# A two-block transformer step on one core: layer-norm statistics by halves on VectorE, and two units of low halves given to GpSimd

## The chip, the cores and the metric

The kernel is one program on one core of one Trainium2 chip. The metric is the device time of one launch in microseconds. The core's engines each run an instruction stream of their own: TensorE (PE; its weight loads PEld), VectorE (DVE), ScalarE (ACT), GpSimd (POOL) and SyncE (SP, here only a DMA queue). They meet through counting semaphores.

## The reference

The input x is 256 tokens by 1024, fp32. The first block has two layers, each with adaptive modulation, a token mixer and a feed-forward part; a second block with RMS norms, half-step feed-forward parts and two more mixers follows. Cut to the part around the change:

```python
def layer_norm(x, g, b):
    mu = xf.mean(-1, keepdims=True)
    var = jnp.square(xf - mu).mean(-1, keepdims=True)
    return ((xf - mu) * lax.rsqrt(var + LN_EPS) * g + b)

def swiglu(h, w_in, w_out):
    g, u = jnp.split(h @ w_in, 2, axis=-1)
    return (jax.nn.silu(g) * u) @ w_out

for l in range(2):
    ada = jax.nn.silu(c) @ w_ada[l] + b_ada[l]
    sh1, sc1, g1, sh2, sc2, g2 = [a[:, None, :] for a in jnp.split(ada, 6, axis=-1)]
    h = x * (1.0 + sc1) + sh1
    y = mixer_ab(h, ...) if l == 0 else mixer_cd(h, ...)
    x = layer_norm(DEEPNORM_ALPHA * x + (1.0 + g1) * y, ln_g[l, 0], ln_b[l, 0])
    h = x * (1.0 + sc2) + sh2
    y = swiglu(h, w_ffn_in[l], w_ffn_out[l])
    x = layer_norm(DEEPNORM_ALPHA * x + (1.0 + g2) * y, ln_g[l, 1], ln_b[l, 1])
```

There are four of these layer norms, numbered e = 0 to 3: e = 0 lies ahead of the first feed-forward part (`ff0`), e = 1 ahead of the second mixer (`cd`), e = 2 ahead of the second feed-forward part (`ff1`), e = 3 ahead of the second block's first feed-forward part (`f1a`).

## The kernel before

**Tiling.** x is kept as two tiles of 128 tokens (tt = 0, 1) by 1024. Every weight matrix is streamed in units of 128 x 2048 fp32 (1 MB). A unit goes through a ring of three slots (`RING`): SP's DMAs bring it into `raw` (L1185, L1211), ScalarE writes its high halves `wH` in a narrower format (`split`, L1458), VectorE the low halves `wL` = raw - wH (`split`, L1895), and TensorE multiplies high by high, high by low and low by high, so that each fp32 product is three matmuls (`half_unit`, L2780, for the gate and up units of a feed-forward part). `hi_ready`, `lo_ready` and `unit_used` count the units at each step; the slot of unit n is n mod 3, and the SP queue refills a slot when TensorE has used it. Units are numbered through the whole program (`START`): ab begins at 0, ff0 at 16, cd at 49, ff1 at 65, f1a at 98.

**Order.** Nothing is scheduled by a planner: each engine's block lists its work in the order in which it is to be issued, and an engine that waits holds back all that stands behind in its list.

**A layer norm.** TensorE leaves y in four banks (tile by half). On VectorE `layer_norm` (L2178) multiplies each half by the gate row (`gated`, L2183), adds it to the scaled x (L2195 for tile 0 in one instruction of 1024, L2201 for tile 1 by halves), takes tile 1's statistics with bn_stats (L2202) and bn_aggr (L2204), and multiplies each tile by its reciprocal root (`normalise`, L2187, L2189, L2191). Tile 0's statistics are ScalarE's: `root` (L1737) makes three passes over it (L1741 to L1743) before the square root (L1744). TensorE transposes the normalised tile (`turn_tile`, L2579), ScalarE applies gain, shift and modulation by columns and writes high halves (`normed_piece`, L1752 and L1761), VectorE writes the low halves of that piece (`lower_piece`, L2242), and TensorE starts the unit's matmuls piece by piece; `keep_busy` (L2564) fills a gap on TensorE with spare matmuls. The columns for e = 0 are made by `join` (L2381 to L2384) from the last `ada` result, which TensorE turns into columns (L2558) and ScalarE copies out (`ada_evac`, L1468).

**The rows of x.** x itself gets ln_g and ln_b later, by rows, in `affine` (L2214 multiplies, L2215 adds, 128 x 1024 each, per tile); no matmul needs it, but the next residual does, and `product` (L2118 in ff0 and ff1, L2116 in f1a) of the feed-forward part stands behind it in VectorE's list. The rows come by GpSimd's DMAs (`load_ln`, L1312 and L1313).

**GpSimd's list.** Around the norms it issues DMAs only: `load_ln`, a table for attention biases (L1321), and `ada` loads (L1274 the bias, L1275 a 2 MB piece of `w_ada` into one of two buffers, `ada_raw`). VectorE sums each piece over its eight chunks in ff0 (`ada`, L1913, and `ada_some`, L1925, `s_late` in the profile) and waits for the load before that.

```python
for l in range(2):
    pool.wait_ge(nat_ready, 2 * TR[("o_ab", "o_cd")[l]] + 2)
    load_ln(l, 0)
    if l == 0:
        pool.dma_start(bias[:, 0:8, :], toep_tile(12, 8)).then_inc(toep_in, 16)
        ada(0, 0, 5120, 32)
        with pool.Fori(0, 2) as m:
            with pool.Fori(0, 4) as j:
                ada(1, 1, m * 3072 + j * 512, (m * 4 + j) * 8 + 48)
```

## Time and profile before

| what | value |
|---|---|
| runs | 1693.11, 1693.89, 1694.65 us (median 1693.89) |
| the profiled execution | 1696.21 us, span 1694.3 us |
| granted TensorE clock, mean | 0.985 |
| PE busy, PEld busy | 1618.3 us (96%), 1351.3 us (80%) |
| DVE, ACT, POOL busy | 1078.5 us (64%), 814.2 us (48%), 224.6 us (13%) |
| SP's queue (q1), GpSimd's queue (q0) | 276.93 MB (48.8% of 16 engines' span), 52.06 MB (8.9%) |

The span is the time from the first to the last recorded instruction of that execution; its own time is 1.9 us longer. All durations quoted below come from this one execution, which lies 2.3 us over the median. Busy shares are means over stages with different limits. Times at the start of a row are microseconds from the start of the span; an "x8" at its end is the number of instructions that the row stands for.

### The profile page before, as it was taken

Reading aid. Unit: us, or ns where it says so; the run is one execution under the profiler, and the core shown is the slowest. Engines: PE = TensorE matmul, PEld = TensorE weight load, DVE = VectorE, ACT = ScalarE, POOL = GpSimd, SP = SyncE. Lnnn points to the kernel's source line nnn. Section 1 sums busy time; section 2 is a strip of 40 time slices with the busy share of each in tenths; the row PEclk is TensorE's granted clock in tenths of the full one; section 3 lists DMA queues with packets and bytes.
Section 4 is the critical chain, followed back from the end, with each engine's and each line's share of the span. In section 5 each row is a group of like instructions: output and inputs, shape, how many; then the busy total and the mean of one; then the engine's idle time right before and its main releaser. Section 6 shows DMA issues by size and latency. Waiting matters only on the chain.

```text
span 1694.3 us, 24620 instructions
## 1 busy us (share of the span) xinstructions
PE 1618.3 (96%) x9255; PEld 1351.3 (80%) x9255; DVE 1078.5 (64%) x1313; ACT 814.2 (48%) x1052; POOL 224.6 (13%) x300
## 2 busy tenths in 40 slices
PE   3999799999998999989999999999999999999999
PEld 2997588877885888868887988888888888878887
DVE  7787777878746545674545986454565456765454
ACT  1564533435655443464445665434454445664433
POOL 2100010000000000048938200000000001300000
PEclk8999899999999999999999999999999999999999
DMA  9974778875543755555553525555555555345552
GB/s 319 336 244 165 253 269 313 285 257 175 190 165 124 258 191 181 182 154 189 183 197 125 168 84 167 200 185 194 178 180 192 185 187 171 128 162 186 187 185 99
DMA packets 225751, 330.10 MB, mean 195 GB/s; under 512 B 10424, under 2 KB 187161, under 8 KB 225679
## 3 DMA queue, kind: packets, MB, share of 16 engines
q1 hardware_dynamic: 210480, 276.93, 48.8%
q0 software_dynamic: 14800, 52.06, 8.9%
q8 instruction: 50, 0.82, 0.2%
q10 hardware_dynamic: 398, 0.11, 0.0%
q14 instruction: 23, 0.18, 0.0%
HBM read 327.97 MB, written 1.09 MB: 194 GB/s over the span
## 4 chain that ended last, share of the span: by engine, by line
PE 76%; DVE 10%; DMA 6%; ACT 4%; issue 2%; SPq 0%; POOLq 0%; DVEq 0%; POOL 0%; ACTq 0%
PE bank L2780 36%; PE bank L2524 22%; PE bank L2512 7%; DMA s_late<-in_w_ada 5%; DVE s_late L1913 4%; PE bank L2482 3%; DVE s_wL L1895 2%; PE bank L2792 1%; ACT s_wH L1458 1%; DMA s_mix<-in_w_ada 1%; PE bank L2494 1%; DVE s_late L1925 1%; DMA s_raw<-in_w_ffn_in 1%; PE bank L2623 1%; PE bank L2579 1%
## 5 line engine op out<-in xcount | busy, mean ns | idle before, releaser
L1895 DVE TENSOR_TENSOR s_wL<-s_raw,s_wH 128x2048 fp32r<-128x2048 f32 x254 | 586.4, 2310 | 290.9 <-ACT s_wH L1458 290.4
L1458 ACT ACTIVATE s_wH<-s_raw 128x2048 fp32r<-128x2048 f32 x254 | 485.1, 1910 | 225.6 <-PE bank L2780 140.2
L2780 PE MATMUL bank<-s_wH,s_hH 128*128 128x512 f32 x1056 | 423.0, 401 | 16.8 <-DVE s_mix L2118 10.4
L2780 PE MATMUL bank<-s_wH,s_hL 128*128 128x512 f32 x1056 | 413.9, 392 | 0.0
L2780 PE MATMUL bank<-s_wL,s_hH 128*128 128x512 f32 x1056 | 413.6, 392 | 0.0
L2780 PEld LDWEIGHTS bank<-s_wH,s_hH 128*128 128x128 f32 x1056 | 199.9, 189 | 62.4 <-issue 18.0
L2780 PEld LDWEIGHTS bank<-s_wH,s_hL 128*128 128x128 f32 x1056 | 199.6, 189 | 43.1
L2780 PEld LDWEIGHTS bank<-s_wL,s_hH 128*128 128x128 f32 x1056 | 200.2, 190 | 40.1 <-issue 0.7
L2524 PE MATMUL bank<-s_wH,s_aH 128*128 128x512 f32 x496 | 195.4, 394 | 1.0 <-DVE s_hL L2017 0.7
L2524 PE MATMUL bank<-s_wH,s_aL 128*128 128x512 f32 x496 | 194.2, 392 | 0.0
L2524 PE MATMUL bank<-s_wL,s_aH 128*128 128x512 f32 x496 | 194.0, 391 | 0.0
L1650 ACT ACTIVATE s_aH<-bank 128x512 fp32r<-128x512 f32 x60 | 35.9, 598 | 225.0 <-PE bank L2792 225.0
L2524 PEld LDWEIGHTS bank<-s_wH,s_aH 128*128 128x128 f32 x496 | 93.8, 189 | 21.0 <-DVE s_hL L2017 0.8
L2524 PEld LDWEIGHTS bank<-s_wH,s_aL 128*128 128x128 f32 x496 | 93.7, 189 | 19.9
L2524 PEld LDWEIGHTS bank<-s_wL,s_aH 128*128 128x128 f32 x496 | 93.8, 189 | 19.2
L2123 DVE TENSOR_TENSOR s_aL<-bank,s_aH 128x512 fp32r<-128x512 f32 x60 | 41.5, 691 | 99.0 <-ACT s_aH L1650 99.0
L1644 ACT ACTIVATE s_mix<-bank,s_small 128x256 f32<-128x256 f32 x88 | 41.8, 475 | 116.1 <-PE bank L2780 116.1
L2512 PE MATMUL bank<-s_hH,s_wH 128*128 128x256 f32 x288 | 84.9, 295 | 4.4 <-DVE s_hL L1930 4.4
L1913 DVE SCALAR_TENSOR_TENSOR s_late<-s_late,s_silc 128x512 f32<-128x512 f32 x94 | 70.7, 752 | 22.9 <-DMA s_late<-in_w_ada 19.8
L2512 PE MATMUL bank<-s_hL,s_wH 128*128 128x256 f32 x288 | 82.6, 287 | 0.0
L2512 PE MATMUL bank<-s_hH,s_wL 128*128 128x256 f32 x288 | 82.5, 287 | 0.0
L2116 DVE SCALAR_TENSOR_TENSOR s_mix<-bank,s_small,s_mix 128x256 f32<-128x256 f32 x88 | 42.3, 481 | 49.3 <-ACT s_mix L1644 49.3
(458 smaller groups left out, 2249.1 us busy)
## 6 DMA issues: line engine op xcount, KB each, us to landing
s_raw<-in_w_ffn_in SPq DMA_DIRECT2D x88, 512.0 KB, 4.9
s_raw<-in_ffn_w_gate SPq DMA_DIRECT2D x88, 512.0 KB, 3.7
...
s_late<-in_w_ada POOLq DMA_DIRECT2D x20, 2048.0 KB, 9.8
...
```

The source lines that it names most:

```text
L1458: A(wH[:, slot, :], raw[:, slot, :], ACT.Copy).then_inc(hi_ready, 1)
L1644: A(sil[:, tt, :], bank[GU_BANK[tt]][:, 0:UC], ACT.Silu, scale=rstd[:, tt:tt + 1] if name in RFFN else 1.0)\
L1650: A(dst, bank[ACT_BANK][:].rearrange("p (a t) -> p a t", a=2), ACT.Copy).then_inc(act_hi, 1)
L1895: TTn(wL[:, slot, :], raw[:, slot, :], wH[:, slot, :].bitcast(F32), ALU.subtract).then_inc(lo_ready, 1)
L1913: STT(acc, src, silc[:, k:k + 1], rows_b if k == 0 else acc, ALU.mult, ALU.add)\
L1925: STT(acc, ada_raw[:, slot, 512 * k:512 * k + 512], silc[:, k:k + 1], ada_b[:, slot, :] if k == 0 else acc, ALU.mult, ALU.add).then_inc(ad ...
L2116: STT(act[:, tt, :], up, rstd[:, tt:tt + 1], sil[:, tt, :], ALU.mult, ALU.mult).then_inc(act_mul, 1)
L2123: TTn(low, bank[ACT_BANK][:].rearrange("p (a t) -> p a t", a=2), high.bitcast(F32), ALU.subtract).then_inc(act_lo, 1)
L2482: last = mm(dst[:, ft * T:ft * T + T], w, h[:, k, :], start=opens(name, ft, k, i), stop=(k == KC - 1 and i == 2), skip_group_check=True)
L2512: last = mm(dst[:, out_c], w, z, start=opens(name, half, k, i), stop=(k == KC - 1 and i == 2), skip_group_check=True)
L2524: last = mm(bank[SUM_BANK[name][2 * tt + h] if name else 2 * tt + h][:], s, w[:, k, c], start=(start and k == 0 and i == 0), stop=(stop an ...
L2780: last = mm(bank[GU_BANK[tt]][:], h, w[:, k, :], start=(half == 0 and k == 0 and i == 0), stop=(half == 1 and k == 3 and i == 2), skip_gro ...
```

## The change

It has five parts.

1. Both tiles of a layer norm are handled in one way on VectorE: gated half, residual half, bn_stats of the half, twice, then bn_aggr and `normalise`; tile 0 is normalised before anything of tile 1 is begun. ScalarE's three passes over tile 0 go.
2. `join` for e = 0 moves from the end of the mixer's list into `layer_norm`, behind tile 0's normalise, with an event "joined" for which ScalarE's first `normed_piece` waits. On TensorE the last `ada` column product moves behind the last output half of the mixer.
3. On ScalarE the high halves of unit START+1 come ahead of the first root (for e = 0 and 2), both pieces of tile 0 ahead of the second root, and the high halves of unit START+2 right behind that.
4. In ff0, ff1 and f1a VectorE no longer makes the low halves of units START+1 and START+2. A new function `lower_units` on GpSimd does, behind `load_ln` in its list.
5. `affine` is split into `gain` and `offset`, and the four passes are placed between the low halves of tile 1's pieces; a wait for unit START+2's low halves stands behind them.

The norm e = 1 takes parts 1 and, in two halves, 5 (in its old order), e = 3 keeps ScalarE's order of root and high halves.

```diff
@@ -1312,9 +1312,18 @@
                 pool.dma_start(lnv[:, 0, :], a["ln_g"][l, n:n + 1, :].to_broadcast([P, D])).then_inc(ln_loaded, 16)
                 pool.dma_start(lnv[:, 1, :], a["ln_b"][l, n:n + 1, :].to_broadcast([P, D])).then_inc(ln_loaded, 16)
 
+            def lower_units(name):
+
+                for n in (START[name] + 1, START[name] + 2):
+                    slot = n % RING
+                    pool.wait_ge(hi_ready, n + 1)
+                    pool.wait_ge(lo_ready, n + LO0)
+                    pool.tensor_tensor(wL[:, slot, :], raw[:, slot, :], wH[:, slot, :].bitcast(F32), ALU.subtract).then_inc(lo_ready, 1)
+
             for l in range(2):
                 pool.wait_ge(nat_ready, 2 * TR[("o_ab", "o_cd")[l]] + 2)
                 load_ln(l, 0)
+                lower_units(("ff0", "ff1")[l])
                 if l == 1:
                     ada(1, 0, 5632, 72)
                 if l == 0:
@@ -1326,6 +1335,8 @@
                     ada(0, 0, 5632, 40)
                 pool.wait_ge(ln_used, 2 * l + 1)
                 load_ln(l, 1)
+                if l == 1:
+                    lower_units("f1a")
                 if l == 0:
                     ada(1, 0, 2048, 48)
                     ada(1, 0, 2560, 56)
@@ -1737,11 +1748,7 @@
             def root(e, tt):
 
                 act_e.wait_ge(var_ready, 2 * e + tt + 1)
-                if tt == 0:
-                    step(A(nat[:, 0, :], x[:, 0, :], ACT.Identity, accum_out=mv[:, 0, 0:1]))
-                    step(A(neg_mean, mv[:, 0, 0:1], ACT.Copy, scale=-1.0 / D))
-                    step(A(nat[:, 0, :], x[:, 0, :], ACT.Square, bias=neg_mean, accum_out=mv[:, 0, 1:2]))
-                A(std[:, tt:tt + 1], mv[:, tt, 1:2], ACT.Sqrt, bias=eps_ln, scale=(1.0 / D, 1.0)[tt]).then_inc(std_ready, 1)
+                A(std[:, tt:tt + 1], mv[:, tt, 1:2], ACT.Sqrt, bias=eps_ln).then_inc(std_ready, 1)
 
             def normed_piece(name, e, tt, half):
 
@@ -1762,14 +1769,19 @@
 
             def normed(name, e):
 
+                if e != 3:
+                    split_py(START[name] + 1)
                 root(e, 0)
-                split_py(START[name] + 1)
+                if e == 3:
+                    split_py(START[name] + 1)
+                if e == 0:
+                    act_e.wait_ge(ev("joined"), 1)
                 normed_piece(name, e, 0, 0)
+                normed_piece(name, e, 0, 1)
                 root(e, 1)
-                normed_piece(name, e, 0, 1)
+                split_py(START[name] + 2)
                 normed_piece(name, e, 1, 0)
                 normed_piece(name, e, 1, 1)
-                split_py(START[name] + 2)
 
             def rms_pieces(name, early):
 
@@ -2097,9 +2109,6 @@
                 lower_direct(7, 3).then_inc(tl_ready, 1)
                 ada_pieces(16)
                 split_py(n0 + 16)
-                if l == 0:
-                    dve.wait_ge(ada_out[1], 7)
-                    join(0, 0, 16)
                 dve.wait_ge(tl_ready, 4 * TR[o] + 4)
                 dve.sem_inc(o_done, 1)
                 dve.sem_inc(nat_ready, 2)
@@ -2185,33 +2194,37 @@
                 def normalise(tt):
                     dve.wait_ge(std_ready, 2 * e + tt + 1)
                     step(dve.reciprocal(rstd[:, tt:tt + 1], std[:, tt:tt + 1]))
+                    TS(x[:, tt, :], x[:, tt, :], mv[:, tt, 0:1], rstd[:, tt:tt + 1], ALU.subtract, ALU.mult).then_inc(nat_ready, 1)
+
+                for tt in range(TT):
+                    for h in range(2):
+                        at = slice(512 * h, 512 * h + 512)
+                        step(gated(tt, h))
+                        if first and (tt, h) == (1, 1):
+                            lower_piece(first, 0, 0)
+                        step(STT(x[:, tt, at], x[:, tt, at], ALPHA, nat[:, tt, at], ALU.mult, ALU.add))
+                        last = dve.bn_stats(stat[:, tt, 6 * h:6 * h + 6], x[:, tt, at])
+                    step(last)
+                    dve.bn_aggr(mv[:, tt, :], stat[:, tt, 0:12].rearrange("p (h s) -> p h s", h=2)).then_inc(var_ready, 1)
                     if tt == 0:
-                        TS(x[:, 0, :], x[:, 0, :], neg_mean, rstd[:, 0:1], ALU.add, ALU.mult).then_inc(nat_ready, 1)
-                    else:
-                        TS(x[:, 1, :], x[:, 1, :], mv[:, 1, 0:1], rstd[:, 1:2], ALU.subtract, ALU.mult).then_inc(nat_ready, 1)
-
-                gated(0, 0)
-                step(gated(0, 1))
-                STT(x[:, 0, :], x[:, 0, :], ALPHA, nat[:, 0, :], ALU.mult, ALU.add).then_inc(var_ready, 1)
-                for h in range(2):
-                    at = slice(512 * h, 512 * h + 512)
-                    step(gated(1, h))
-                    if h:
                         normalise(0)
-                    step(STT(x[:, 1, at], x[:, 1, at], ALPHA, nat[:, 1, at], ALU.mult, ALU.add))
-                    last = dve.bn_stats(stat[:, 1, 6 * h:6 * h + 6], x[:, 1, at])
-                step(last)
-                dve.bn_aggr(mv[:, 1, :], stat[:, 1, 0:12].rearrange("p (h s) -> p h s", h=2)).then_inc(var_ready, 1)
+                    if (e, tt) == (0, 0):
+                        dve.wait_ge(ada_out[1], 7)
+                        join(0, 0, 16)
+                        dve.sem_inc(ev("joined"), 1)
                 if first:
-                    lower_piece(first, 0, 0)
+                    lower_piece(first, 0, 1)
                 normalise(1)
 
-            def affine(e, tt):
+            def gain(e, tt):
 
                 if tt == 0:
                     dve.wait_ge(ln_loaded, 32 * (e + 1))
                 dve.wait_ge(tr_done, TRD[LN_TR[e]] + (4 if LN_TR[e] == "cd" else 2 * tt + 2))
                 step(TTn(x[:, tt, :], x[:, tt, :], lnv[:, 0, :], ALU.mult))
+
+            def offset(e, tt):
+
                 TTn(x[:, tt, :], x[:, tt, :], lnv[:, 1, :], ALU.add).then_inc(ev("x_done"), 1)
                 if tt == 1:
                     dve.wait_ge(ev("x_done"), 2 * e + 2)
@@ -2396,25 +2409,21 @@
                     transposed(name, lambda c: lnS[:, e, c:c + 1], lambda c: lnS[:, e, 8 + c:9 + c], whole=False)
                     split_py(START[name] + 1)
                     split_py(START[name] + 2)
-                    affine(e, 0)
-                    affine(e, 1)
+                    for tt in range(TT):
+                        gain(e, tt)
+                        offset(e, tt)
                     return
                 layer_norm(e, gate, y, name)
-                split_py(START[name] + 1)
-                lower_piece(name, 0, 1)
-                if name == "f1a":
-                    affine(e, 0)
+                gain(e, 0)
+                offset(e, 0)
                 lower_piece(name, 1, 0)
+                gain(e, 1)
                 lower_piece(name, 1, 1)
-                if name != "f1a":
-                    split_py(START[name] + 2)
-                    affine(e, 0)
-                affine(e, 1)
+                offset(e, 1)
                 if name == "f1a":
                     row_scale(name, 0)
                     row_scale(name, 1)
-                    split_py(START[name] + 2)
-
+                dve.wait_ge(lo_ready, START[name] + 2 + (LO0 + 1))
 
             e = 0
             for l, (p, o, f) in enumerate((("ab", "o_ab", "ff0"), ("cd", "o_cd", "ff1"))):
@@ -2764,9 +2773,9 @@
                 values(7)
                 out_half(2, 1, (1,))
                 out_half(3, 0)
+                out_half(3, 1)
                 if l == 0:
                     ada_turn(*ADA_LAST, 2)
-                out_half(3, 1)
 
             def ffn(name, after=None, with_ada=False):
                 n0, f, ready = START[name], 11 * FFN[name], 4 * TR[name]
```

(Left out of the diff is a renaming of a local helper `gain` to `by_gain` in two loops.)

The change in line numbers: VectorE's low halves are L1907, a gated half L2192, the reciprocal L2196, normalise L2197, the residual half L2205, bn_stats L2206, bn_aggr L2208, gain L2224, offset L2228, a low piece L2255, `join` L2394 to L2397, the `ada` sums L1925 (loop) and L1937; ScalarE's high halves L1469, root L1751, a piece L1759 and L1768; GpSimd's subtraction L1321 and the table's load L1330.

GpSimd's list at the norm e = 0, before (`s_mix` holds the rows of ln_g and ln_b and the bias table, `s_late` the `ada` buffers):

```order
L1312 DMA s_mix<-in_ln_g 128x1024 [waits nat_ready]
L1313 DMA s_mix<-in_ln_b 128x1024
L1321 DMA s_mix<-toep_scratch 128x8x256
L1274 DMA s_late<-in_b_ada 1x16x32 [waits ada_step0]
L1275 DMA s_late<-in_w_ada 128x8x512
```

and with the change:

```order
L1312 DMA s_mix<-in_ln_g 128x1024 [waits nat_ready]
L1313 DMA s_mix<-in_ln_b 128x1024
L1321 ISA
L1321 TENSOR_TENSOR s_wL<-s_raw,s_wH 128x2048 [waits lo_ready,hi_ready] x2
L1330 DMA s_mix<-toep_scratch 128x8x256
L1274 DMA s_late<-in_b_ada 1x16x32 [waits ada_step0]
L1275 DMA s_late<-in_w_ada 128x8x512
```

Two subtractions, each waiting for `hi_ready` and `lo_ready`, now stand between the row loads and the three DMAs that follow.

VectorE's list at e = 0, before, from the low halves of unit 16 (first row) to tile 0's normalise and the next half (last rows); `s_t` is the gated half, `s_x` the residual sum:

```order
L1895 TENSOR_TENSOR s_wL<-s_raw,s_wH 128x2048 [waits hi_ready]
L2381 TENSOR_SCALAR s_adaC<-s_adaC 128x8 [waits ada_out1]
L2382 TENSOR_TENSOR s_lnS<-s_lnC,s_adaC 128x8 [waits v_step]
L2383 TENSOR_TENSOR s_lnS<-s_lnC,s_adaC 128x8 [waits v_step]
L2384 TENSOR_TENSOR s_lnS<-s_lnS,s_adaC 128x8 [waits v_step]
L2183 TENSOR_TENSOR s_t<-bank,s_gate 128x512 [waits v_step,tl_ready,y_part,ada_out0]
L2183 TENSOR_TENSOR s_t<-bank,s_gate 128x512 [waits y_part]
L2195 SCALAR_TENSOR_TENSOR s_x<-s_x,s_t 128x1024 [waits v_step]
L2183 TENSOR_TENSOR s_t<-bank,s_gate 128x512 [waits y_part]
L2201 SCALAR_TENSOR_TENSOR s_x<-s_x,s_t 128x512 [waits v_step]
L2202 BN_STATS s_small<-s_x 128x6 [waits v_step]
L2183 TENSOR_TENSOR s_t<-bank,s_gate 128x512 [waits unit_used]
```

and with the change:

```order
L1907 TENSOR_TENSOR s_wL<-s_raw,s_wH 128x2048 [waits hi_ready]
L2192 TENSOR_TENSOR s_t<-bank,s_gate 128x512 [waits tl_ready,y_part,ada_out0]
L2205 SCALAR_TENSOR_TENSOR s_x<-s_x,s_t 128x512 [waits v_step]
L2206 BN_STATS s_small<-s_x 128x6 [waits v_step]
L2192 TENSOR_TENSOR s_t<-bank,s_gate 128x512 [waits y_part]
L2205 SCALAR_TENSOR_TENSOR s_x<-s_x,s_t 128x512 [waits v_step]
L2206 BN_STATS s_small<-s_x 128x6 [waits v_step]
L2208 BN_AGGR s_small<-s_small 128x2 [waits v_step]
L2196 RECIPROCAL s_small<-s_small 128x1 [waits std_ready]
L2197 TENSOR_SCALAR s_x<-s_x,s_small 128x1024 [waits v_step]
L2394 TENSOR_SCALAR s_adaC<-s_adaC 128x8 [waits ada_out1]
L2395 TENSOR_TENSOR s_lnS<-s_lnC,s_adaC 128x8 [waits v_step]
```

The wait for `ada_out1` has moved from ahead of the norm to behind tile 0's normalise, and tile 0 goes through bn_stats and bn_aggr with nothing of tile 1 between.

VectorE's list behind tile 1's normalise (`s_hL` is a piece of low halves of the activations, `s_wL` a unit's), before:

```order
L1895 TENSOR_TENSOR s_wL<-s_raw,s_wH 128x2048 [waits hi_ready]
L2242 TENSOR_TENSOR s_hL<-s_mix,s_hH 128x4x128 [waits th_ready] x3
L1895 TENSOR_TENSOR s_wL<-s_raw,s_wH 128x2048 [waits hi_ready]
L2214 TENSOR_TENSOR s_x<-s_x,s_mix 128x1024 [waits tr_done,ln_loaded]
L2215 TENSOR_TENSOR s_x<-s_x,s_mix 128x1024 [waits v_step]
L2214 TENSOR_TENSOR s_x<-s_x,s_mix 128x1024 [waits tr_done]
L2215 TENSOR_TENSOR s_x<-s_x,s_mix 128x1024 [waits v_step]
L2118 TENSOR_TENSOR s_mix<-bank,s_mix 128x256 [waits e_x_done,sil_done]
```

and with the change:

```order
L2224 TENSOR_TENSOR s_x<-s_x,s_mix 128x1024 [waits tr_done,ln_loaded]
L2228 TENSOR_TENSOR s_x<-s_x,s_mix 128x1024 [waits v_step]
L2255 TENSOR_TENSOR s_hL<-s_mix,s_hH 128x4x128 [waits th_ready]
L2224 TENSOR_TENSOR s_x<-s_x,s_mix 128x1024 [waits tr_done]
L2255 TENSOR_TENSOR s_hL<-s_mix,s_hH 128x4x128 [waits th_ready,v_step]
L2228 TENSOR_TENSOR s_x<-s_x,s_mix 128x1024
L2127 TENSOR_TENSOR s_mix<-bank,s_mix 128x256 [waits e_x_done,sil_done,lo_ready]
```

The two units are gone, and the affine passes stand around the two low pieces of tile 1.

## Rows read from the trace of the kernel before

**Rows 1.** The page, part 4: the chain's shares by engine.

```profile
PE 76%; DVE 10%; DMA 6%; ACT 4%; issue 2%; SPq 0%; POOLq 0%; DVEq 0%; POOL 0%; ACTq 0%
```

**Rows 2.** Chain (start, us, what), 164 to 215; by line, 205 to 345.

```profile
165.22 0.80 PE bank L2558 x8
...
174.17 1.97 PE bank L2579 x8
...
190.82 1.23 DVE s_x L2214
...
196.41 7.56 PE bank L2780 x24
...
by line: DMA s_late<-in_w_ada 49.0%; DVE s_late L1913 34.3%; issue 8.3%; DVE s_late L1925 2.2%; DVE s_wL L1895 1.6%; PE bank L2780 1.5%; POOLq L1274 0.8%; PE bank L2925 0.6%; DVE s_mix L2118 0.5%; PE bank L2792 0.5%; ACT s_aH L1650 0.4%; PO
```

**Rows 3.** Timeline of VectorE, 163 to 215: start, length, line, shapes.

```profile
163.15 2.29 DVE L1895 TENSOR_TENSOR s_wL<-s_raw,s_wH 128x2048 fp32r<-128x2048 f32 x1
...
170.56 0.69 DVE L2201 SCALAR_TENSOR_TENSOR s_x<-s_x,s_t 128x512 f32<-128x512 f32 x1
171.28 0.69 DVE L2202 BATCH_NORM_STATS2 s_small<-s_x 128x6 f32<-128x512 f32 x1
171.89 0.67 DVE L2183 TENSOR_TENSOR s_t<-bank,s_gate 128x512 f32<-128x512 f32 x1
...
205.69 6.25 DVE L1913 SCALAR_TENSOR_TENSOR s_late<-s_late,s_silc 128x512 f32<-128x512 f32 x8
```

**Rows 4.** Timeline of ScalarE, 163 to 200.

```profile
166.23 1.28 ACT L1735 ACT_TABLE_LOAD   x1
...
171.43 1.15 ACT L1743 ACTIVATE s_t<-s_x,s_small 128x1024 f32<-128x1024 f32 x1
```

**Rows 5.** Groups by form, GpSimd: shapes, count | busy us, mean ns.

```profile
L1417 POOL TENSOR_TENSOR s_late<-s_mix 128x512 f32<-128x512 f32 x8 | 10.4, 1296 | 0.6
...
L1166 POOL TENSOR_TENSOR s_late<-s_mix 128x1020 f32<-128x1020 f32 x1 | 1.9, 1885 | 0.1
...
L1349 POOL TENSOR_TENSOR s_mix<-s_mix 128x256 f32<-128x256 f32 x1 | 0.7, 742 | 0.1
```

**Rows 6.** Timeline of GpSimd and VectorE, 842 to 895.

```profile
847.68 0.69 DVE L2123 TENSOR_TENSOR s_aL<-bank,s_aH 128x512 fp32r<-128x512 f32 x1 [1.91 <-ACT s_aH L1650]
...
887.79 1.05 POOL L1415 TENSOR_TENSOR s_mix<-s_mix,s_s5c 128x512 f32<-128x512 f32 x1 [28.15 <-ACT s_mix L1718]
...
890.06 1.30 POOL L1417 TENSOR_TENSOR s_late<-s_mix 128x512 f32<-128x512 f32 x1
891.43 2.98 POOL L1415 TENSOR_TENSOR s_mix<-s_mix,s_s5c 128x512 f32<-128x512 f32 x1
...
890.52 2.98 DVE L1895 TENSOR_TENSOR s_wL<-s_raw,s_wH 128x2048 fp32r<-128x2048 f32 x1 [5.14 <-ACT s_wH L1458]
```

**Rows 7.** DMA issues from 171 to 173: KB, us to landing.

```profile
s_late<-in_w_ada POOLq DMA_DIRECT2D x1, 2048.0 KB, 20.8
```

**Rows 8.** Windows: us; busy PE, PEld, DVE, ACT, POOL; clock; DMA; GB/s.

```profile
184.00:188.00 4.00, 4.00 (x19) 3.16 (x18) 1.39 (x2) 3.94 (x8) 0.00 (x0) 1.00 1.02 392
545.00:548.00 3.00, 2.89 (x7) 2.34 (x8) 3.00 (x3) 0.00 (x0) 0.00 (x0) 0.52 0.03 5
```

**Rows 9.** Timeline of VectorE at the norm into cd, of ScalarE in f1a.

```profile
383.27 1.29 DVE L2183 TENSOR_TENSOR s_t<-bank,s_gate 128x512 f32<-128x512 f32 x2
...
392.15 0.81 DVE L2191 TENSOR_SCALAR s_x<-s_x,s_small 128x1024 f32<-128x1024 f32 x1
...
740.32 1.06 ACT L1789 ACTIVATE s_mix<-s_x 128x1024 f32<-128x1024 f32 x1
...
743.48 1.90 ACT L1458 ACTIVATE s_wH<-s_raw 128x2048 fp32r<-128x2048 f32 x1
```

**Rows 10.** Chain of waits, where ff1 and f1a start their second unit.

```profile
545.11 7.32 PE bank L2780 x24
...
748.16 3.04 PE bank L2780 x12
```

More of the change, by code:

```diff
@@ L1864, in _ @@
             for l, (f1, p, o, f2) in enumerate((("f1a", "even", "o_even", "f2a"), ("f1b", "odd", "o_odd", "f2b"))):
-                gain = lambda at, l=l: (lambda c: cols[:, at + 8 * l + c:at + 8 * l + c + 1])
+                by_gain = lambda at, l=l: (lambda c: cols[:, at + 8 * l + c:at + 8 * l + c + 1])
                 if l == 0:
@@ L1872, in _ @@
                 ffn(f1)
-                rms_turned(p, gain(C_MIX), l == 1)
+                rms_turned(p, by_gain(C_MIX), l == 1)
                 if l == 0:
@@ L2440, in _ @@
                 residual(f1)
-                rms_turned(p, gain(C_MIX), l == 1)
+                rms_turned(p, by_gain(C_MIX), l == 1)
                 if l == 0:
```

2 lines of the change are left out of this document (1 added, 1 removed).

## The prediction, made blind

> **What bounds the kernel now.** I read the page's chain of waits first, then the chain piece by piece, then each place that the diff touches in order of time. TensorE is 76% of the chain, VectorE 10% [rows 1]: only a stretch in which TensorE waits can give or lose anything. The four layer norms are such stretches. Around the first one (into ff0) the chain leaves TensorE at 166.0, behind the eight small matmuls of the last `ada` piece, runs over VectorE, ScalarE's statistics and VectorE's normalise to the transposes at 174.17, comes back to VectorE at 190.82 for four affine passes, and ends with the product (L2118) that lets the second unit start at 196.41 [rows 2]. Behind it follows a second chain: from 205 to 345 us it is 49% DMA of `in_w_ada` and 34% the VectorE sums over it (L1913) [rows 2], so ff0 is paced by when those loads land, the first sum starting at 205.69 [rows 3].
>
> **The price of the parts.** VectorE: a gated half 0.67, a half of the residual sum 0.69, bn_stats 0.69 (the next, independent instruction starts 0.61 after its start, a dependent one 0.03 after its end), low halves of a unit 2.29 [rows 3], an affine pass 1.23 [rows 2], normalise 0.81 [rows 9]. ScalarE: the second of the removed passes 1.15, a table load 1.28 [rows 4], high halves of a unit 1.90 [rows 9].
> The new instruction is GpSimd's 128x2048 subtraction; no row of it exists. Nearest is L1417, two SBUF inputs, 128x512: 1.30; L1349 with 128x256: 0.742 [rows 5]. That is 2.19 ns per element, so 1.30 + 1536 x 0.00219 = 4.66; I take 4.6. The lower end is L1166, two inputs of 1020 elements in 1.885 [rows 5]: 3.8 in proportion, a little less if part of it is fixed, so 3.6.
> The Trainium skill's page "GPSIMD Engine Reference", section 3.1, gives 4.497 us for a two-input op of 2048 elements; by it the sum below would be some 0.6 us smaller.
>
> **What VectorE and GpSimd do to each other.** GpSimd's L1417 runs 890.06 to 891.36. VectorE's L1895, begun at 890.52, takes 2.98 in place of 2.29, as if it started at 891.3; GpSimd's next, begun at 891.43, takes 2.98 where L1415 alone takes 1.05, and ends 1.0 behind VectorE's end [rows 6]. Who starts first holds the other for its whole instruction. The sum of bank and high halves (L2123) at 847.68 keeps its 0.69 beside a running GpSimd [rows 6]. So I take residual sums, affine passes, lower pieces, low halves and, less surely, normalise as held, gated halves and bn_stats as free. The rows show a hold of at most 1.3 us; mine is 4.6, an extrapolation.
> The Trainium skill's "SBUF — State Buffer", section "Who interferes with whom", states that rule: the pair is a lock for the whole instruction, the second to issue is blocked fully, and a two-port op such as normalise is held too. The trace agrees as far as it goes (0.7 us of delay on L1895). By the rows alone, three holds of at most 1.3 us would leave the second rival below near -2 us; by the rule the forecast stands.
>
> **ff0 (e = 0).** VectorE no longer waits for `join`: the first gated half starts at 165.4, where the unit's low halves end [rows 3]. One tile costs 2.05 + 2.15 + 0.25 = 4.45, so the variance is there at 169.85. But ScalarE is late: the last `ada` column product now stands behind `out_half(3, 1)`, which ends near 168.0 without it, so its evacuation (166.04 before) comes near 169.1, then the table 1.28 and 0.2, then high halves of unit 17, 170.7 to 172.6, and only then the root. GpSimd's first subtraction starts at 172.7 on those high halves; normalise wants to start at 173.1. It is held to 177.3 and ends at 178.0, against 174.1 before, where the transposes follow at 174.17 [rows 2].
> From there by the same prices: piece (0,0) of the low halves 182.0, tile 1 normalised 185.2. The first affine pass starts 185.1; GpSimd's second subtraction (high halves ready 185.8) gets in at 186.3, behind it, and holds the next pass from 186.4 to 190.8. Piece (1,0) lands at 192.6, TensorE's last two half units take 2.73 each and end at 198.1, and the second half unit behind it starts at 200.8, where the same walk of before puts it at 199.0: +1.9.
> Then the queue. Behind the two subtractions on GpSimd stand the Toeplitz load and two `ada` loads. Before, an `ada` load issued at 171.4 took 20.8 us to land [rows 7], 13 us before it was wanted; now the second one issues at 193.6, behind the lock's end at 190.8 and 2.8 us of issuing. DMA ran at 392 GB/s then [rows 8]; ahead of landing are some 5 MB of this queue and 2 MB of weights, 7 / 0.39 = 18 us: 211. VectorE would want it at 205.69 + 1.9 = 207.6. The sum starts at 211, and since this chain paces ff0 [rows 2], the whole is +5.2. With 3.6 us the same walk gives 208, +2.1.
>
> **cd (e = 1).** No GpSimd work. Before: from 383.27 to tile 1 normalised at 392.96, 9.7 [rows 9], with ScalarE's statistics beside VectorE's second tile. After: both tiles in a row on VectorE, 4.45 + 0.35 + 0.2 + 0.8 each, 11.6, and ScalarE's root of tile 1 and the unit's high halves behind it, which gate its pieces, move with it. +1.9.
>
> **ff1 (e = 2).** High halves of unit 66 come first, 515.2 to 517.1, so GpSimd starts by 517.1 to 517.7, against the first tile's second residual half: that sum waits from 519.0 to 522.2, and normalise ends near 525.2, some 1.4 later than before. The second subtraction again takes the lock between the affine passes (532.6 to 533.1, held to 537.6). But the four affine passes and 2.29 of low halves no longer stand ahead of the product: TensorE's last half unit ends 544.9, where the product let it start at 545.11 [rows 10]. 0; with 3.6 us, -2.
> The 24 matmuls from there took 7.32 [rows 10], at first at a granted clock of 0.52, the 1.2 GHz level [rows 8], behind 5.2 us of idleness; the 12 at 748.16 took 3.04 [rows 10], by which 24 take 6.1. The idle gap shrinks to 3.6 us, so up to 1.2 may come back. I keep that for the range.
>
> **f1a (e = 3).** The first tile is normalised 1.9 earlier, at 723.7. The first subtraction (high halves 724.5) then holds piece (0,0) from 727.0 to 729.5, the second the second affine pass from 734.5 to 739.0. The offset of tile 1 ends at 743.8; behind it stand ScalarE's square, table load, silu and high halves, 745.38 - 740.32 = 5.1 [rows 9], then 2.29 of VectorE and the product, which releases TensorE at 751.4. Before, that product released it at 748.16 [rows 10]; my walk of before puts it at 747.8: +3.6. With 3.6 us, +1.6.
>
> **Costed at nothing:** removed ScalarE statistics, 4 x 3 us, since VectorE now waits for its own; bn_stats (2 more per norm) are in the 4.45. What is lost is the cover of the `ada` loads, those 13 us.
>
> **Sum:** 5.2 + 1.9 + 0 + 3.6 = +10.7. On the profiled execution's 1696.21 (span 1694.3) this is 1706.9; the median of the runs is 2.3 lower, so 1704.6.
>
> **Rivals.** *Shorter holds* (0.23): 3.6 us, and loads nearly in time: 2.1 + 1.9 - 2.0 + 1.6 = +3.6, 1697.5. For it: L1166's slope. Against: L1417's.
> *No hold* (0.16): a 2048-element instruction shares the ports, or VectorE wins each start (in ff0 it would have to be 0.45 us earlier). Place: the three feed-forward norms. The same walk without holds releases TensorE 4.2, 6.6 and 2.5 us earlier; in ff0 the loads still land at 207, +1.5. So 1.5 + 1.9 - 6.6 - 2.5 = -5.7, 1688.2. It decides if VectorE's stretching is under about 1 us per subtraction. Against: [rows 6].
> *Loads collide* (0.10): the `ada` loads meet the weight units too, so ScalarE waits for raw weights at 200 to 212; 3 to 5 us more, 1708.5.
>
> **Numbers.** Forecast 0.51. What a measurement of this kernel can tell from no change is about 0.2%, 3.4 us, so 1690.5 to 1697.3 is "same". Faster takes the third rival; same takes a third of the first; slower the rest. Likeliest 1704.6; the low end 1692 lies halfway between the first rival with 1.2 of clock back and the second, the high end 1710 above the third.
>
> **Signs.** Right: L1321 on GpSimd about 4.6 us, its second one longer; VectorE's first normalise (L2197) some 4.9 in ff0; an affine pass of 5 to 6 us three times; L1925's wait on `in_w_ada` before the loop; tile 1 of cd later by 1.9. Wrong: L1321 above 5.5 or below 3; affine passes all at 1.22; the chain through ff0 starting its DMA pieces no later than 213.

## The result and the profile after

The changed kernel takes 1704.25 us (median of 6 runs, 1703.51 to 1707.13) against 1694.27 for the kernel before (6 runs, three of them those of the table above, 1691.61 to 1698.68). The ratio is 1.0059, 95% interval 1.0043 to 1.0074: slower by 10 us. The profiled executions are 1703.51 and 1696.21 us; they differ by 7.3 only, because the one of before was late when it left the first mixer (below).

The page of the changed kernel, busy time and the chain by engine, as [rows 1]:

```profile
PE 1619.9 (95%) x9255; PEld 1353.9 (80%) x9255; DVE 1094.2 (64%) x1323; ACT 805.0 (47%) x1032; POOL 253.4 (15%) x306
...
PE 82%; DVE 9%; DMA 4%; ACT 3%; issue 2%; SPq 0%; POOL 0%; DVEq 0%; POOLq 0%; ACTq 0%
```

VectorE is busy 16 us longer although six units' low halves (6 x 2.29 = 14 us) left it. It is waiting inside its instructions: the six that meet a subtraction are 22 us longer than alone. GpSimd's timeline (start, us, line):

```profile
170.19 4.49 POOL L1321 TENSOR_TENSOR s_wL<-s_raw,s_wH 128x2048 fp32r<-128x2048 f32 x1 [8.49 <-ACT s_wH L1469]
183.31 4.84 POOL L1321 TENSOR_TENSOR s_wL<-s_raw,s_wH 128x2048 fp32r<-128x2048 f32 x1 [8.64 <-ACT s_wH L1469]
...
190.95 0.95 POOL L1275 DMA_DIRECT2D s_late<-in_w_ada  x1
...
521.69 4.96 POOL L1321 TENSOR_TENSOR s_wL<-s_raw,s_wH 128x2048 fp32r<-128x2048 f32 x1 [1.58 <-ACT s_wH L1469]
537.52 4.82 POOL L1321 TENSOR_TENSOR s_wL<-s_raw,s_wH 128x2048 fp32r<-128x2048 f32 x1 [10.86 <-ACT s_wH L1469]
...
729.02 4.86 POOL L1321 TENSOR_TENSOR s_wL<-s_raw,s_wH 128x2048 fp32r<-128x2048 f32 x1 [161.28 <-ACT s_wH L1469]
738.20 4.85 POOL L1321 TENSOR_TENSOR s_wL<-s_raw,s_wH 128x2048 fp32r<-128x2048 f32 x1 [4.33 <-ACT s_wH L1469]
```

and VectorE's beside it, the held rows and some that are not:

```profile
170.52 4.71 DVE L2197 TENSOR_SCALAR s_x<-s_x,s_small 128x1024 f32<-128x1024 f32 x1
...
183.74 5.49 DVE L2228 TENSOR_TENSOR s_x<-s_x,s_mix 128x1024 f32<-128x1024 f32 x1
...
210.65 6.27 DVE L1925 SCALAR_TENSOR_TENSOR s_late<-s_late,s_silc 128x512 f32<-128x512 f32 x8 [6.17 <-DMA s_late<-in_w_ada]
...
398.08 0.81 DVE L2197 TENSOR_SCALAR s_x<-s_x,s_small 128x1024 f32<-128x1024 f32 x1
...
523.58 3.62 DVE L2205 SCALAR_TENSOR_TENSOR s_x<-s_x,s_t 128x512 f32<-128x512 f32 x1
...
537.94 5.48 DVE L2228 TENSOR_TENSOR s_x<-s_x,s_mix 128x1024 f32<-128x1024 f32 x1
...
729.54 0.69 DVE L2206 BATCH_NORM_STATS2 s_small<-s_x 128x6 f32<-128x512 f32 x1
730.15 0.67 DVE L2192 TENSOR_TENSOR s_t<-bank,s_gate 128x512 f32<-128x512 f32 x1
731.26 3.16 DVE L2255 TENSOR_TENSOR s_hL<-s_mix,s_hH 128x512 fp32r<-128x512 f32 x1 [0.44 <-ACT s_hH L1768]
...
738.64 5.49 DVE L2228 TENSOR_TENSOR s_x<-s_x,s_mix 128x1024 f32<-128x1024 f32 x1
```

Each long row ends 0.5 to 1.1 us behind the end of GpSimd's, a little less than the 0.69 to 1.22 us that it takes alone: 170.19 + 4.49 = 174.68, and the normalise that was issued at 170.52 ends at 175.23. Normalise, residual sum, offset and low piece are held; bn_stats and the gated half, which reads a bank, keep 0.69 and 0.67 in the middle of a subtraction (729.54 and 730.15 lie between 729.02 and 733.88). The chain of waits runs over the load that stood behind both subtractions:

```profile
190.95 19.55 DMA s_late<-in_w_ada
210.65 0.76 DVE s_late L1925
```

And TensorE stands still for it. On ScalarE (ACT), VectorE and TensorE, in this order of time:

```profile
211.87 1.92 ACT L1469 ACTIVATE s_wH<-s_raw 128x2048 fp32r<-128x2048 f32 x1 [2.84 <-DMA s_raw<-in_w_ffn_in]
...
216.83 2.28 DVE L1907 TENSOR_TENSOR s_wL<-s_raw,s_wH 128x2048 fp32r<-128x2048 f32 x1
...
219.83 1.12 PE L2801 MATMUL bank<-s_ident,s_mix 128*128 128x128 f32 x4 [5.79 <-DVE s_mix L2127]
```

The sum of eight chunks ends at 216.92, the low halves and the product follow, and TensorE has waited 5.79 by then. The kernel before has no wait of this kind here.

The ledger for all runs: the length of each stage in the profiled execution in us, from rows of the timelines. ff0: from the first spare matmul behind the first mixer to the first gated half of the norm into cd. cd and ff1: from there to the first gated half of the next norm. The rest: from the norm into f1a to VectorE's last instruction.

| kernel | ff0 | cd | ff1 | f1a and the rest |
|---|---|---|---|---|
| before | 214.5 | 133.1 | 201.5 | 973.4 |
| changed | 221.0 | 133.5 | 201.5 | 976.4 |
| changed, again | 221.5 | 135.8 | 203.1 | 976.4 |
| loads first, two runs | 215.5, 214.0 | 138.1, 134.5 | 201.5, 201.7 | 976.4, 976.4 |
| VectorE's low halves | 208.3 | 135.7 | 194.9 | 971.8 |
| the same, cd as before | 209.6 | 133.2 | 195.3 | 971.8 |
| GpSimd's part alone | 226.3 | 132.3 | 206.6 | 983.0 |
| cd as before | 221.2 | 133.3 | 201.5 | 976.4 |
| statistics alone | 214.3 | 134.1 | 200.2 | 971.8 |
| affine order alone | 207.2 | 134.9 | 195.6 | 973.3 |
| four pieces | 226.7 | 134.6 | 197.1 | 976.0 |
| tile 1 later, new and old statistics in the feed-forward norms | 210.7, 211.2 | 136.1, 133.2 | 194.6, 196.3 | 971.9, 974.2 |

The last column repeats to 0.1 between kernels that are alike there (with one exception, 973.3 and 974.2 for the two with the affine order alone in f1a), ff0 and ff1 to about 1.6, cd only to several. So the change costs 6.5 in ff0, 0.4 in cd, 0 in ff1 and 3.0 in f1a, 9.9 in all; by the second execution of the changed kernel it is 7.0, 2.7, 1.6 and 3.0. The first mixer is all but untouched by the change (eight small products of TensorE change places, and the spare matmuls stand behind them in both), and its end was at 168.74 in the execution of before, at 166.30 in the changed one; that 2.4 is why the two profiled executions lie closer together than the medians.

The same stages seen from TensorE: how long it stood idle, in us, and the mean granted clock (f1a: its first 45 us only).

| kernel | ff0 | cd | ff1 | f1a |
|---|---|---|---|---|
| before | 11.7, 0.96 | 7.1, 0.99 | 8.3, 0.98 | 6.6, 1.00 |
| changed | 17.5, 0.95 | 7.6, 0.99 | 7.3, 0.97 | 7.4, 0.92 |
| loads first, second run | 13.5, 0.97 | 8.6, 0.97 | 7.7, 0.97 | 6.9, 0.92 |
| VectorE's low halves | 9.7, 0.99 | 8.6, 0.97 | 4.1, 1.00 | 4.9, 1.00 |
| GpSimd's part alone | 22.1, 0.94 | 6.6, 0.99 | 11.4, 0.97 | 12.3, 0.85 |
| affine order alone | 7.9, 0.98 | 7.5, 0.97 | 5.0, 1.00 | 6.5, 1.00 |

Idle time is only a part of what a stage loses. Against the version with VectorE's low halves, GpSimd's part costs 6.6 in ff1, of which 3.2 are idle time of TensorE; in the rest TensorE does the same work (861 matmuls in each of the four executions compared here), but slower, at a granted clock that falls to the 1.2 GHz level behind a wait. The 5.9 that the affine order alone gains in ff1 divide in the same way, 3.3 of idle time and 2.6 of slower work.

### The profile page after: what moved, and what is told of

The parts are those of the page before. It is cut to its first block, busy times and chain, and to the rows that moved or that the text cites. A ratio compares the mean times of both kernels' runs of the same rounds, so it can differ in the third digit from the quotient of the medians.

```text
span 1701.8 us, 24629 instructions
## 1 busy us (share of the span) xinstructions
PE 1619.9 (95%) x9255; PEld 1353.9 (80%) x9255; DVE 1094.2 (64%) x1323; ACT 805.0 (47%) x1032; POOL 253.4 (15%) x306
## 4 chain that ended last, share of the span: by engine, by line
PE 82%; DVE 9%; DMA 4%; ACT 3%; issue 2%; SPq 0%; POOL 0%; DVEq 0%; POOLq 0%; ACTq 0%
PE bank L2789 39%; PE bank L2533 24%; PE bank L2521 7%; PE bank L2491 3%; PE bank L2801 2%; DMA s_late<-in_w_ada 2%; DVE s_wL L1907 2%; DVE s_late L1925 1%; ACT s_wH L1469 1%; DMA s_mix<-in_w_ada 1%; PE bank L2503 1%; DMA s_raw<-in_w_ffn_in 1%; PE bank L2632 1%; DVE s_x L2228 1%; DVE s_late L1937 1%
## 5 line engine op out<-in xcount | busy, mean ns | idle before, releaser
L1907 DVE TENSOR_TENSOR s_wL<-s_raw,s_wH 128x2048 fp32r<-128x2048 f32 x248 | 572.7, 2310 | 297.0 <-ACT s_wH L1469 296.4
L1469 ACT ACTIVATE s_wH<-s_raw 128x2048 fp32r<-128x2048 f32 x254 | 485.1, 1910 | 217.0 <-PE bank L2789 160.6
L2789 PEld LDWEIGHTS bank<-s_wH,s_hL 128*128 128x128 f32 x1056 | 200.2, 190 | 43.2
L1925 DVE SCALAR_TENSOR_TENSOR s_late<-s_late,s_silc 128x512 f32<-128x512 f32 x94 | 70.7, 752 | 13.9 <-DMA s_late<-in_w_ada 10.9
```

The lines of the kernel that those rows point to most:

```text
L1469: A(wH[:, slot, :], raw[:, slot, :], ACT.Copy).then_inc(hi_ready, 1)
L1907: TTn(wL[:, slot, :], raw[:, slot, :], wH[:, slot, :].bitcast(F32), ALU.subtract).then_inc(lo_ready, 1)
L1925: STT(acc, src, silc[:, k:k + 1], rows_b if k == 0 else acc, ALU.mult, ALU.add)\
L2789: last = mm(bank[GU_BANK[tt]][:], h, w[:, k, :], start=(half == 0 and k == 0 and i == 0), stop=(half == 1 and k == 3 and i == 2), skip_gro ...
```

## The experiments

**1. The queue on GpSimd.** It takes the changed kernel and issues the loads before the subtractions in ff0:

```diff
                 load_ln(l, 0)
-                lower_units(("ff0", "ff1")[l])
                 if l == 1:
+                    lower_units("ff1")
...
                     ada(0, 0, 5120, 32)
-                    with pool.Fori(0, 2) as m:
-                        with pool.Fori(0, 4) as j:
-                            ada(1, 1, m * 3072 + j * 512, (m * 4 + j) * 8 + 48)
+                    ada(1, 1, 0, 48)
+                    lower_units("ff0")
+                    with pool.Fori(1, 4) as j:
+                        ada(1, 1, j * 512, j * 8 + 48)
+                    with pool.Fori(0, 4) as j:
+                        ada(1, 1, j * 512 + 3072, j * 8 + 80)
```

> The changed kernel, but in ff0 GpSimd issues the table load and the two ada loads before its two subtractions. Theory (the loads behind the subtractions cost ff0 its time): the second ada load is issued near 171 again instead of 190.95, lands near 192, the first sum of ff0 starts near 204.5 instead of 210.65, and the time is 5 us below the changed kernel's, near 1699. Rival (the holds themselves set ff0's length, the loads are late only beside them): the second unit and all behind it move by less than 1 us, 1703.5 or more.

Measured: 1699.49 us (12 runs, 1694.26 to 1705.29), ratio 1.0002 [0.9979, 1.0026]. Run again beside the changed kernel:

> The changed kernel as it is, to stand beside the loads-first version on one chip. Theory: 0.6% above the kernel before, as in its first runs.

> The loads-first version once more, since its first runs fell in two groups (1694 to 1698 and 1701 to 1705) and its profiled execution was of the upper one. Theory: 4 to 5 us under the changed kernel in the median; a profiled execution shows ff0's end 4 to 5 us earlier, and where it is of the upper group the difference is lost in the second mixer, not in a feed-forward norm.

Measured on that chip: changed 1706.27 us, ratio 1.0045 [1.0029, 1.0061]; loads first 1697.82, ratio 1.0000 [0.9985, 1.0014]. VectorE's timeline of the second loads-first run, with GpSimd's above it:

```profile
164.76 0.93 POOL L1275 DMA_DIRECT2D s_late<-in_w_ada  x1
170.44 4.49 POOL L1321 TENSOR_TENSOR s_wL<-s_raw,s_wH 128x2048 fp32r<-128x2048 f32 x1 [4.75 <-ACT s_wH L1472]
...
204.06 0.69 DVE L2135 TENSOR_TENSOR s_aL<-bank,s_aH 128x512 fp32r<-128x512 f32 x1 [2.00 <-ACT s_aH L1664]
204.67 6.25 DVE L1928 SCALAR_TENSOR_TENSOR s_late<-s_late,s_silc 128x512 f32<-128x512 f32 x8
```

The wait of 6.17 on `in_w_ada` is gone: the second load is issued at 164.76 in place of 190.95. ff0 takes 5.5 and 7.5 less than in the two changed executions (221.0 - 215.5, 221.5 - 214.0), the other stages keep their lengths, but for the cd stage, which took 138.1 in the first run, 2 to 6 longer than elsewhere, so that run lost its gain in the second mixer. It is the granted clock that differs there:

```profile
387.32:520.81 133.49, 125.84 (x914) 107.48 (x913) 93.24 (x191) 75.09 (x145) 3.93 (x6) 0.99 0.50 166
...
382.74:520.84 138.10, 129.95 (x913) 111.13 (x913) 93.25 (x192) 75.06 (x145) 3.92 (x6) 0.95 0.49 160
```

(windows of the cd stage, columns as in [rows 8], the changed kernel above, the first loads-first run below: TensorE is busy 4.1 us longer over the same matmuls, at 0.95 in place of 0.99, and idle 0.5 longer). What decides which of the two an execution gets is not settled. In the medians the queue is worth 4.8 us, between sessions, and 8.5 on one chip.

With the loads first, ff0 takes 215.5 and 214.0, the kernel before 214.5: there the held instructions cost about what the new order gains, and the loss against before is the late load.

**2. GpSimd's part taken away.** Against the changed kernel, `lower_units` is not called; VectorE does

```diff
                 layer_norm(e, gate, y, name)
+                split_py(START[name] + 1)
                 gain(e, 0)
...
-                dve.wait_ge(lo_ready, START[name] + 2 + (LO0 + 1))
+                split_py(START[name] + 2)
```

> The changed kernel without GpSimd's subtractions: VectorE makes the low halves of both units again (unit START+1 behind tile 1's normalise, unit START+2 behind the affine passes), the statistics and the new order stay. Theory (GpSimd's part costs, the statistics nearly nothing): normalise in ff0 back to 0.81, no affine pass over 1.3, ff0 2 below before, ff1 1 to 2 below, f1a within 1 of before, in all 1690 to 1693. Rival (VectorE's serial statistics are the cost): above 1699.

Measured: 1683.04 us, ratio 0.9903 [0.9866, 0.9939]. Its first normalise and join:

```profile
172.78 0.81 DVE L2194 TENSOR_SCALAR s_x<-s_x,s_small 128x1024 f32<-128x1024 f32 x1
173.51 0.17 DVE L2391 TENSOR_SCALAR s_adaC<-s_adaC 128x8 f32<-128x8 f32 x1
```

The direction was right and the size wrong: I expected 1690 to 1693. By the medians GpSimd's six subtractions cost 21 us, and what is left of the change gains 11 (14 against the before of its own session, 1696.66). By stage, against the changed execution, GpSimd costs 12.7 in ff0, 6.6 in ff1 and 4.6 in f1a, with cd 2.2 the other way, within its scatter.

**3. GpSimd's part alone,** put into the kernel before (the same function and calls, VectorE's three `split_py` lines for these units in `normed` dropped, the wait for unit START+2 at its end).

> The kernel before, with nothing changed but that GpSimd makes the low halves of units START+1 and START+2 in ff0, ff1 and f1a. Theory: the loads behind it cost ff0 4 to 5 us, and one or two held passes in each of the three norms cost as much as VectorE saves; 1699 to 1703. Rival (it is only the new order that lets GpSimd take the lock at a bad moment): within 1 us of 1694 apart from ff0's loads, so 1698 at most. VectorE's second tile (residual sum or normalise) should show 3 to 4 us beside the first subtraction, an affine pass 4 to 6 beside the second.

Measured: 1720.72 us, ratio 1.0129 [1.0091, 1.0167], 24 us over the before of its session and 18 beyond what I expected at most. Its rows at f1a:

```profile
740.34 4.56 POOL L1321 TENSOR_TENSOR s_wL<-s_raw,s_wH 128x2048 fp32r<-128x2048 f32 x1 [162.75 <-ACT s_wH L1469]
...
742.87 2.57 DVE L2253 TENSOR_TENSOR s_hL<-s_mix,s_hH 128x512 fp32r<-128x512 f32 x1 [1.38 <-ACT s_hH L1772]
...
757.72 5.63 DVE L2226 TENSOR_TENSOR s_x<-s_x,s_mix 128x1024 f32<-128x1024 f32 x1
```

The affine pass has the expected length, and it was a low piece and not the second tile that met the first subtraction. Low piece and last affine pass both stand on the path there. The low piece ends 1.9 late, TensorE stands idle 3.44 us for it, where it was 1.56 before, and then works at the lower clock level (windows behind the low piece, this run above, before below; the clock is the third number from the right):

```profile
745.50:751.60 6.10, 6.01 (x18) 4.82 (x19) 3.79 (x5) 0.01 (x1) 0.00 (x0) 0.54 0.53 175
...
729.40:735.00 5.60, 5.56 (x28) 4.69 (x29) 5.56 (x5) 3.41 (x9) 0.00 (x0) 1.00 0.19 53
```

The 12 matmuls ahead of tile 1's transposes take 5.25 us in place of 2.85, so a piece that was 1.9 late makes the second tile 4.3 late, ahead of the held affine pass. My walk had no such term. GpSimd's part costs no less in the old order than in the new one, 24 us against 21; only in f1a is the new order kinder to it (4.6 against 9.6).

**4. The norm into cd.** Changed kernel, e = 1 as before (ScalarE's three passes, old order of VectorE):

```diff
+                if (e, tt) == (1, 0):
+                    step(A(nat[:, 0, :], x[:, 0, :], ACT.Identity, accum_out=mv[:, 0, 0:1]))
+                    step(A(neg_mean, mv[:, 0, 0:1], ACT.Copy, scale=-1.0 / D))
+                    step(A(nat[:, 0, :], x[:, 0, :], ACT.Square, bias=neg_mean, accum_out=mv[:, 0, 1:2]))
...
```

> The changed kernel with the norm into cd as it was (ScalarE's three passes over tile 0, VectorE's two tiles overlapped). The changed kernel's tile 1 was normalised 1.9 us later there, but the second mixer gave 1.4 of it back before ff1. By that 0.4 us are gained, 1703.8; by the step of the prediction that charged all 1.9, 1702.3.

> The changed kernel without GpSimd's subtractions and with the norm into cd as it was before. From the version without GpSimd's subtractions alone (1683.0) cd's part should come back: it was 2.7 us over the kernel before between the end of ff0 and the first gated half of ff1. Theory: 1680 to 1681. Rival (the second mixer absorbs it, as the run of the changed kernel with the old cd norm suggested): 1683.

Measured: 1704.30 us, ratio 1.0038 [1.0018, 1.0059], and with VectorE's low halves 1681.07, ratio 0.9901 [0.9882, 0.9921], against 0.9903 for the one without. Neither can be told from its partner. In the changed execution tile 1 was normalised 11.57 behind the first gated half (387.32 to 398.89), before it was 9.69 [rows 9], so the 1.9 is there; over the seven executions of the table with VectorE's statistics at cd the stage has a mean of 135.2 (133.5 to 138.1), over the seven with the old ones 133.7 (132.3 to 136.1). The lengths overlap because the clock differs between executions; TensorE's idle time in the stage does not overlap, 7.6 to 8.6 (mean 8.3) with VectorE's statistics and 6.1 to 7.5 (mean 6.8) with the old ones. So some 1.5 of the 1.9 reach TensorE, too little for the medians to show.

**5. Statistics or order.** Each put alone into the kernel before; with the statistics, ScalarE's second piece of tile 0 also goes ahead of the second root, and VectorE's second low piece ahead of tile 1's normalise.

> The kernel before with VectorE's statistics alone (both tiles by halves, ScalarE's three passes gone); affine passes, join, GpSimd and high halves where they were. The version with all but GpSimd's part gained 11 to 13 us. Theory (the affine passes' new places brought that, not the statistics): tile 0 normalised about 1 us earlier and tile 1 no earlier in the feed-forward norms, 2 to 3 lost at cd; 1692 to 1696 against 1694. Rival (the statistics brought it): under 1689.

> The kernel before with only the four affine passes moved in between the low halves of tile 1's pieces (no new statistics, no GpSimd work). Theory: in ff0 and ff1 the four passes (4.9 us) no longer stand between the low halves of unit START+2 and the product, each gains 4 to 5, f1a under 1; 1684 to 1687. Rival (statistics): above 1691.

The second one is

```diff
                 layer_norm(e, gate, y, name)
                 split_py(START[name] + 1)
                 lower_piece(name, 0, 1)
-                if name == "f1a":
-                    affine(e, 0)
+                gain(e, 0)
+                offset(e, 0)
                 lower_piece(name, 1, 0)
+                gain(e, 1)
                 lower_piece(name, 1, 1)
+                offset(e, 1)
                 if name != "f1a":
                     split_py(START[name] + 2)
-                    affine(e, 0)
-                affine(e, 1)
```

Measured: statistics alone 1692.98 us, ratio 0.9972 [0.9961, 0.9982]; order alone 1682.36, ratio 0.9908 [0.9889, 0.9928]. Both stage by stage: the statistics gain 1.4 in ff1 and 1.6 in f1a, the order 7.3 in ff0 and 5.9 in ff1 and nothing in f1a. The order's part is more than the 4 to 5 expected, since the passes' 4.9 us were not all: in ff1 the 24 matmuls behind the wait for them took 7.32 [rows 10], partly at the lower clock. The chain of the order-alone kernel at the second unit:

```profile
186.59 1.81 ACT s_wH L1458
188.42 2.29 DVE s_wL L1895
190.71 0.34 DVE s_mix L2118
191.10 3.06 PE bank L2784 x12
```

The four passes that stood here from 190.82 to 195.7 [rows 2] are gone from it; they run while TensorE and ScalarE make tile 1's pieces.

**6. Shorter instructions on GpSimd.** The changed kernel with

```diff
-                    pool.tensor_tensor(wL[:, slot, :], raw[:, slot, :], wH[:, slot, :].bitcast(F32), ALU.subtract).then_inc(lo_ready, 1)
+                    for q in range(4):
+                        at = slice(512 * q, 512 * q + 512)
+                        last = pool.tensor_tensor(wL[:, slot, at], raw[:, slot, at], wH[:, slot, at].bitcast(F32), ALU.subtract)
+                    last.then_inc(lo_ready, 1)
```

> The changed kernel with each of GpSimd's 128x2048 subtractions cut in four of 512 columns (1.1 to 1.3 us each). Theory (one of the two engines is held for the other's whole instruction, by turns): normalise in ff0 under 2.2 in place of 4.71, no affine pass over 2.6 in place of 5.49, the pieces between VectorE's passes up to 2.5 each; ff1 and f1a end 2 to 4 earlier each, the loads in ff0 stay late; 1697 to 1700. Rival (they share bandwidth, so the same bytes cost VectorE the same time however cut): 1703 to 1705, normalise still over 4.

Measured: 1706.52 us, ratio 1.0050 [1.0033, 1.0067].

```profile
170.22 5.38 POOL L1323 TENSOR_TENSOR s_wL<-s_raw,s_wH 128x512 fp32r<-128x512 f32 x4 [8.49 <-ACT s_wH L1472]
183.22 6.74 POOL L1323 TENSOR_TENSOR s_wL<-s_raw,s_wH 128x512 fp32r<-128x512 f32 x4 [7.62 <-ACT s_wH L1472]
...
170.55 1.47 DVE L2200 TENSOR_SCALAR s_x<-s_x,s_small 128x1024 f32<-128x1024 f32 x1
171.94 1.24 DVE L2397 TENSOR_SCALAR s_adaC<-s_adaC 128x8 f32<-128x8 f32 x1
173.22 1.18 DVE L2398 TENSOR_TENSOR s_lnS<-s_lnC,s_adaC 128x8 f32<-128x8 f32 x1
174.43 1.19 DVE L2399 TENSOR_TENSOR s_lnS<-s_lnC,s_adaC 128x8 f32<-128x8 f32 x1
...
183.66 2.19 DVE L2231 TENSOR_TENSOR s_x<-s_x,s_mix 128x1024 f32<-128x1024 f32 x1
```

The shapes are those of turns (normalise 1.47, offset 2.19), which sharing of bandwidth would not give; the time is no better than uncut and near the rival's, for another reason. ff1 gains 4.4, f1a only 0.4, and ff0 loses 5.7: `join`'s three little operations, 0.17 each, now wait 1.2 each for a piece, so VectorE is released no earlier (first gated half of tile 1 at 175.97, against 176.06 uncut), and GpSimd, delayed itself between pieces, issues its second load at 192.76. By that the first sum starts at 213.28 in place of 210.65; the other 3 us come behind it, among the later loads, and their cause stays open.

**7. Tile 1's passes still later,** behind the first two products of ff0 and ff1 and no longer between the low pieces there: once in the version with VectorE's low halves and cd as before, once in the affine order alone.

```diff
                 split_py(n0 + 3)
                 product(0, 1)
+                if name in ("ff0", "ff1"):
+                    gain(2 * (name == "ff1"), 1)
                 split_py(n0 + 4)
+                if name in ("ff0", "ff1"):
+                    offset(2 * (name == "ff1"), 1)
```

> The version with VectorE's low halves and cd's old norm (1681.1), and in ff0 and ff1 the two affine passes of tile 1 moved on, behind the first two products. Theory: in ff0 the unit's high halves no longer wait for the product behind an affine pass, and VectorE is idle there while TensorE works; ff0 gains 1 to 2.5, ff1 nothing (TensorE runs without a gap there), 1679 to 1680. Rival (hidden(0) now comes late): 1683.

> The kernel before with the affine passes interleaved (1682.4) and tile 1's two moved on behind the first two products. There the chain into the second unit runs over ScalarE's table load and high halves, not over the passes. Theory: no change, 1681.5 to 1683. If ff0 is paced by VectorE after all: 1680.

Measured: 1683.70 us, ratio 0.9912 [0.9889, 0.9935], and 1685.01, ratio 0.9919 [0.9897, 0.9940]: nothing gained in either. The versions with the interleaved passes and no work on GpSimd take 1681 to 1685 us, and from these runs they can't be put in an order; the statistics alone come next (1692.98).

## Why the prediction was right

**The sum.** 1704.6 was forecast, 1704.25 measured. By its own terms: ff0 +5.2 forecast, 6.5 measured; cd +1.9, 0.4; ff1 0, 0.0; f1a +3.6, 3.0. In all 10.7 and 9.9. That the total is so near is in part luck: the errors of the terms, 1.3 too little and 1.5 and 0.6 too much, cancel, and by the second execution of the changed kernel (7.0, 2.7, 1.6, 3.0) the sum would be 14.3. What was right is the mechanism, the held instructions and the late load.

**The price of the subtraction.** 4.6 was taken; undisturbed it took 4.49, and 4.82 to 4.96 where VectorE's instruction was ahead of it. The lower end, 3.6, and with it the first rival, is out. The Trainium skill's figure ("GPSIMD Engine Reference", section 3.1, 4.497 us) agrees to 0.01.

**The hold.** It was extrapolated from a hold of at most 1.3 us; it goes on to 4.4 as well. Normalise shows 4.71 where 4.9 was forecast, an affine pass 5.48 or 5.49 three times, as forecast, the residual sum 3.62, and which operations are free came out as chosen. The Trainium skill's rule ("SBUF — State Buffer", section "Who interferes with whom": an exclusive lock for the whole instruction, by order of issue) agrees with all of these, and with the pieces: with the subtraction cut in four, VectorE waits for one piece (1.47 in place of 4.71). That rules out the second rival as a mechanism. The third rival, weight units late in ff0, did come about, but off the path: ScalarE waits 2.84 for a unit before 211.87, has its high halves at 213.79, and VectorE, busy with the sum, takes them up at 216.83 only. In the loads-first runs ScalarE has no such wait until 225.

**The queue.** The forecast was that the first sum waits for a load that stands behind the subtractions; the row at 210.65 shows it, and issuing the loads first removes it. The size was off: the load took 19.55 us, where 17.4 was taken (193.6 to 211), since the queues moved 363 GB/s between 191 and 210.5 and not 392. Counted from the first spare matmul the sum starts 7.4 us later than before (44.35 against 36.95), where 5.3 was forecast; that ff0 began 2.4 us earlier in this execution is how 210.65 came out so near to 211. And the term's parts were wrong: 1.9 were for the holds, net of what the new order gives, and 3.3 for the load, while with the loads first ff0 was as long as before within its scatter.

**ff1 and the clock.** The 0 was right by two errors that cancel. TensorE's last half unit was to end 28.6 us behind the first gated half (544.9 in the times of before); it ended at 30.5 (551.28 in those of the changed kernel), 1.7 later than the product had let it start before (28.8). The second unit's 24 matmuls then took 5.6 in place of 7.32, because the low clock had been spent on the half unit ahead of them: the idle gap shrank from 5.17 to 3.09 (3.6 was forecast), but the clock stayed down for as long as before (windows as in [rows 8], before above and changed below):

```profile
545.00:549.00 4.00, 3.89 (x10) 3.16 (x11) 4.00 (x3) 0.00 (x0) 0.00 (x0) 0.57 0.14 29
...
545.00:549.00 4.00, 4.00 (x13) 3.12 (x12) 2.41 (x4) 0.26 (x1) 0.00 (x0) 0.57 0.50 169
```

So in sum the 1.2 us kept for the range did not come back. They do where the wait goes: with the affine order alone and with VectorE's low halves the granted clock of ff1 is 1.00.

**cd.** The serial statistics cost the 1.9 forecast at tile 1's normalise; TensorE's idle time has some 1.5 of it, averaged over all executions, though the pair compared above shows 0.4.

**What it missed.** The sum counted only differences of the whole and never priced the order of the affine passes by itself, and it had the clock in ff1 only. The walk without holds released TensorE 4.2, 6.6 and 2.5 us earlier and charged 1.5 for late loads; in the run without GpSimd's part ff1 gained 6.7, as that walk had it, and ff0 6.2, since its loads were in time; f1a gained 1.6 only, where the walk had 2.5. So a change that is slower by 10 us is a gain of 11 to 14 and a loss of 21 or more, and the first part was in the working, but not named as a result. My later expectations erred in the same way: for the version without GpSimd's part by 7 us too little gain, for GpSimd's part alone by 18 us too little loss.
